# Odd projection of a hybrid decoder step: outputs stored in two runs a group, and a lighter hand-over to the next stage

## The chip, the cores and the metric

The program runs on one core of one Trainium2 chip. The metric is device time in microseconds (us) of one execution, lower is better; the kernel before takes 3164.81 us, the median of three runs.

## The reference, cut to what matters

One step of a two-layer decoder for 2048 prompt rows and 8 sample rows (2056 columns), D = 1024. The change lies in layer 1, at its input projection and the samples' stick-breaking attention:

```python
proj = x @ w_in                                  # x: 2056 rows of 1024
k_all = concat([cache_k[pages], k_new])          # 4096 past rows for each of 8 samples
z = q @ k_all.T / sqrt(64) + bias                # 8 heads
excl = exclusive_suffix_sum(log_sigmoid(-z))
att = exp(log_sigmoid(z) + excl)
o_c = att @ v_all
out = concat([o_c * silu(g_c), ...]) @ w_out
```

All is float32. The projection is computed as three float32r products of high and low parts.

## The kernel before, in words

`program` runs stages one after the other; each `Stage` ends with all engines at a barrier. Three classes of names matter: `po_` is the odd projection with the samples' attention (`project_odd`, L2448), `pv_` the next stage (`project_values`, L3049), `scratch_` and `out_` lie in device memory.

**The projection.** `Channels` (L1243) computes the transposed product in slots. A slot is one group of 128 output channels (`n`) times one block of 412 columns (`b`, five to a group; the last has 408). `ODD_GROUPS` (L2441) gives the order: slots 0 to 19 are broken up so that queries come early, and from slot 20 on each group's blocks 0 to 4 follow each other, so the block is the slot modulo 5. PE makes 24 matmuls a slot into one of five banks `acc`. ACT copies the bank to `ot` (`evict`, L1362), a buffer of four pieces of 412 columns that slots use in turn, and stores the piece (`store`, L1307). Before it overwrites a piece it waits until the store of four slots ago has landed (`stored`, L1313). There are 105 slots and 105 stores.

**The samples' attention** is spread over the same slots by a table written by hand (L2480 to L2490). Sample b (0 to 7) has its chain at slot c = 22 + 10b. DVE multiplies key pages with the query and reduces them, 16 pairs of pages a sample (`scores`). Then, in the order of the table: ACT takes `po_e` = exp (after its copy of slot c), DVE clamps, ACT takes the logarithm `po_softplus` (after slot c+1), DVE finishes `po_softplus`, PE makes the sums `po_stat` with a triangle and with ones (after slot c+2), DVE makes the argument, ACT takes `po_att` = exp (after slot c+3), and PE multiplies `po_att` with value pages into `po_sums`, from slot c+4 on, eight groups of four pages a sample.

**Queues.** SP issues the key pages. ACT issues the value pages (`load_pages`, L2493: for each page a register load from the page table, register arithmetic and one DMA), the output stores, and the weights of the projection. All this stands in ACT's one instruction stream, between its copies and exponentials. In the loop at L2596 a slot of ACT is: copy, store, weights at the first slot of a group, value pages, exponential or logarithm. POOL splits the weights of later groups into high and low parts.

**The hand-over.** After the last slot SP issues `ValuesAhead.load` (L2741): tile 0 of `pv_x`, four (`FRONT`) of the eight 512 KB parts of `pv_w`, and tile 1 of `pv_x`. Then it stores the samples' output `po_oc` to `scratch_cat` and waits until that has landed. In the next stage SP issues the other four parts, ACT makes `pv_w_high`, DVE first splits `pv_x` tile 0 (`split_x`, L2751) and then makes the eight `pv_w_low`; PE starts with part 0 and needs one part after the other. POOL makes the low half of tile 1, and PE goes on with it.

Of the kernel before, what the change touches and what calls it, by code (L numbers as in the profile page):

```python
# [22 lines left out]
P = 128  # L23
# [1219 lines left out]
class Channels:  # L1243
# [7 lines left out]
    def __init__(self, s, xT, w, out, groups, banks, pinned=False):  # L1251
# [14 lines left out]
        self.kept = [s.sem(f"kept{n}") for n in range(self.PIECES)]  # L1266
# [3 lines left out]
        for t, (i, n, b) in enumerate(self.slot):  # L1270
            self.begin.setdefault(i, t)
        self.opens = {t: i for i, t in self.begin.items()}
        self.at = {(n, b): t for t, (i, n, b) in enumerate(self.slot)}

    def place(self, stage=None):
        s = self.s
        if self.pinned:
            s.sb("fence", [P, 2 * KT * COLS])
        else:
            self.stage = stage  # L1280
            self.xh, self.xl = s.sb("x_high", [P, KT, COLS]), s.sb("x_low", [P, KT, COLS])
            self.wr = s.sb("w", [P, KT * P])
            self.wh, self.wl = s.sb("w_high", [P, 2, KT * P]), s.sb("w_low", [P, 2, KT * P])
        self.ot = s.sb("o", [P, self.PIECES, BLK])
        self.acc = [s.ps(f"acc{n}", [P, 512]) for n in range(self.banks)]

# [1161 lines left out]
def project_odd(nc, xT, w, z, cache_k, cache_v, table, bias, const, q_rows, cat, values_ahead):  # L2448
# [7 lines left out]
    with Stage(nc, "po") as s:  # L2456
# [16 lines left out]
         o_ev, o_pe, gate, out, stored) = (s.sem(n) for n in (  # L2473
             "cst", "tab", "q_tr", "q_ev", "q_st", "set", "prod", "k_used", "v_used", "biased", "exp", "cl", "ln",
             "sp", "tri_pe", "own", "arg", "att", "o_ev", "o_pe", "gate", "out", "stored"))
# [24 lines left out]
        def _(sp):  # L2500
# [33 lines left out]
            sp.dma_start(cat[0:4, :, SEQ:COLS].rearrange("n p c -> p n c"), oc[:, :, :]).then_inc(stored, 16)  # L2534
            sp.wait_ge(stored, 16)
# [51 lines left out]
        def _(act):  # L2587
# [8 lines left out]
            for t in range(TAIL):  # L2596
                if t < pj.slots:
# [6 lines left out]
                    pj.evict(act.copy, act, t, more)  # L2604
                    pj.store(act, t)
# [21 lines left out]
            for t in range(pj.slots - pj.PIECES, pj.slots):  # L2627
                pj.stored(act, t)

        @block.vector  # L2630
        def _(dve):
# [62 lines left out]
            for t in range(START, TAIL):  # L2694
# [10 lines left out]
                if t - PER - 3 in chain:  # L2705
# [4 lines left out]
                              gc[:, :, :].rearrange("p n b -> p (n b)"), ALU.mult).then_inc(out, 1)  # L2710

# [6 lines left out]
class ValuesAhead:  # L2718

    FRONT = 4  # L2720

    def __init__(self, nc, x, w):
# [9 lines left out]
        self.x_high, self.x_low = s.sem("x_high"), s.sem("x_low")  # L2732
# [8 lines left out]
    def load(self, sp):  # L2741
        self.tile(sp, 0)
        for k in range(self.FRONT):
            self.weights(sp, k)
        self.tile(sp, 1)
# [303 lines left out]
def project_values(nc, ahead, out, z, alpha_w, alpha_b, const, ops, wc, sample_vecs, scores):  # L3049
# [6 lines left out]
    with ahead.s as s:  # L3056
# [29 lines left out]
        def _(sp):  # L3086
# [13 lines left out]
            for k in range(ahead.FRONT, KT):  # L3100
                ahead.weights(sp, k)
            for dst, src in ((wt[:, :], alpha_w), (bt[:, :], alpha_b), (mask[:, :], const["reset"][:, 0:GW]),
# [27 lines left out]
            sp.wait_ge(late, 48)  # L3130
            for q in (0, 1):
# [104 lines left out]
        def _(dve):  # L3236
# [53 lines left out]
            ahead.split_x(dve)  # L3290
# [451 lines left out]
```

## Time and profile before

| | |
|---|---|
| median of three runs | 3164.81 us (3162.14 to 3166.29) |
| the profiled execution: its own time | 3165.45 us |
| its span in the profile | 3163.7 us |
| PE busy | 2913.2 us, 92% |
| DVE, ACT, POOL busy | 66%, 41%, 23% |
| stage `po`: first and last matmul of a slot | 1509.0 and 2124.2 us |
| first matmul of stage `pv` | 2141.12 us |

Times in the profile count from the span's start. "Idle" is time of an engine before an instruction, with what ended it. "issue" as a releaser means that the engine waited for nothing that the profile shows: its own instruction stream had other things ahead, here the issuing of DMAs. A granted clock (PEclk) of 1.00 is 2.4 GHz of TensorE, 0.50 is 1.2 GHz.

### The profile page before, as it was taken

Reading aid. Unit: us, or ns where it says so; the run is one execution under the profiler, and the core shown is the slowest. Engines: PE = TensorE matmul, PEld = TensorE weight load, DVE = VectorE, ACT = ScalarE, POOL = GpSimd, SP = SyncE. Lnnn points to the kernel's source line nnn. Section 1 sums busy time; section 2 is a strip of 40 time slices with the busy share of each in tenths; the row PEclk is TensorE's granted clock in tenths of the full one; section 3 lists DMA queues with packets and bytes.
Section 4 is the critical chain, followed back from the end, with each engine's and each line's share of the span. In section 5 each row is a group of like instructions: output and inputs, shape, how many; then the busy total and the mean of one; then the engine's idle time right before and its main releaser. Section 6 shows DMA issues by size and latency. Waiting matters only on the chain. (4 is left out here: it accounts for less than half of the span.)

```text
span 3163.7 us, 70060 instructions
## 1 busy us (share of the span) xinstructions
PE 2913.2 (92%) x27683; PEld 2367.9 (75%) x27683; DVE 2101.6 (66%) x3283; ACT 1291.1 (41%) x2293; POOL 724.9 (23%) x697
## 2 busy tenths in 40 slices
PE   8999999978898988998899999989989999998898
PEld 7899999967776766776887777877756666667676
DVE  9526666647666647885487677604639888887576
ACT  2225555434444435342310100012228888875332
POOL 5000000012232211110011111101227666664111
PEclk9999999989999989999999999999989999999999
DMA  6624545454443556552789999865450101008342
GB/s 214 204 95 151 154 151 153 140 162 117 105 116 87 130 150 195 158 174 84 260 253 342 319 330 322 294 192 170 149 193 6 68 14 55 15 20 257 124 158 77
DMA packets 470335, 502.83 MB, mean 159 GB/s; under 512 B 200065, under 2 KB 362866, under 8 KB 464986
## 3 DMA queue, kind: packets, MB, share of 16 engines
q1 hardware_dynamic: 373466, 339.83, 35.8%
q10 hardware_dynamic: 88032, 142.51, 13.0%
q0 software_dynamic: 8512, 16.02, 1.7%
q8 instruction: 221, 3.62, 0.5%
q14 instruction: 104, 0.85, 0.1%
HBM read 357.13 MB, written 141.31 MB: 158 GB/s over the span
## 5 line engine op out<-in xcount | busy, mean ns | idle before, releaser
L3029 POOL TENSOR_TENSOR sp_att<-sp_beta,sp_left 128x512 f32<-128x512 f32 (+3 forms) x320 | 302.3, 955 | 187.0 <-DVE sp_left L2990 172.6
L120 PE MATMUL po_acc<-po_x_high,po_w_low 128*128 128x412 f32 (+1 forms) x840 | 306.6, 365 | 15.1 <-DVE po_x_low L113 13.7
L120 PE MATMUL pe_acc<-pe_x_high,pe_w_low 128*128 128x412 f32 (+1 forms) x840 | 302.6, 360 | 5.4 <-PEq L86 5.4
L121 PE MATMUL po_acc<-po_x_low,po_w_high 128*128 128x412 f32 (+1 forms) x840 | 299.5, 357 | 0.0
L122 PE MATMUL po_acc<-po_x_high,po_w_high 128*128 128x412 f32 (+1 forms) x840 | 298.7, 356 | 0.0
L121 PE MATMUL pe_acc<-pe_x_low,pe_w_high 128*128 128x412 f32 (+1 forms) x840 | 293.7, 350 | 0.0
L122 PE MATMUL pe_acc<-pe_x_high,pe_w_high 128*128 128x412 f32 (+1 forms) x840 | 293.3, 349 | 0.0
L2990 DVE TENSOR_TENSOR_SCAN sp_left<-sp_z,sp_left,sp_zero 128x512 f32<-128x512 f32 x192 | 235.7, 1269 | 18.3 <-ACT sp_z L2951 14.0
L2654 DVE TENSOR_TENSOR po_work<-po_work,po_q 128x1024 f32<-128x1024 f32 x128 | 177.6, 1388 | 83.3 <-DMA po_work<-in_cache_k 74.4
L2943 ACT ACTIVATE sp_beta<-sp_z,sp_bias 128x512 f32<-128x512 f32 (+3 forms) x320 | 183.1, 628 | 94.1 <-PE sp_z L2881 47.7
L1371 ACT COPY po_o<-po_acc 128x412 f32<-128x412 f32 (+1 forms) x105 | 52.5, 500 | 392.2 <-PE po_acc L122 337.2
L120 PEld LDWEIGHTS po_acc<-po_x_high,po_w_low 128*128 128x128 f32 x840 | 162.4, 193 | 65.2 <-issue 33.1
L2430 POOL TENSOR_TENSOR rc_kt<-rc_kt,rc_mask 128x512 f32<-128x512 f32 x32 | 41.4, 1294 | 716.5 <-ACT rc_kt L2320 716.4
L2316 ACT COPY rc_lv<-rc_bk 128x1024 f32<-128x1024 f32 (+1 forms) x192 | 129.9, 693 | 181.1 <-DVE rc_f L2406 54.6
L2892 PEld LDWEIGHTS sp_t<-sp_id,sp_att 128*128 128x128 f32 x1088 | 117.4, 141 | 96.8 <-issue 89.8
L2951 ACT ACTIVATE sp_z<-sp_z,sp_bias_neg 128x512 f32<-128x512 f32 (+3 forms) x320 | 179.2, 610 | 0.0
L120 PEld LDWEIGHTS pe_acc<-pe_x_high,pe_w_low 128*128 128x128 f32 x840 | 158.4, 189 | 17.7 <-issue 16.5
L2878 PE MATMUL sp_z<-sp_k,sp_q 64*128 64x512 f32 (+3 forms) x640 | 164.0, 589 | 6.5 <-PEq L86 3.3
L2892 PE MATMUL sp_t<-sp_id,sp_att 128*128 128x128 f32 x1088 | 152.2, 279 | 17.5 <-ACT sp_aT L2957 16.6
L121 PEld LDWEIGHTS po_acc<-po_x_low,po_w_high 128*128 128x128 f32 x840 | 162.6, 194 | 0.9
L122 PEld LDWEIGHTS po_acc<-po_x_high,po_w_high 128*128 128x128 f32 x840 | 162.4, 193 | 0.7
L2909 PE MATMUL sp_ob<-sp_aT,sp_v 128*64 128x128 f32 x2176 | 154.7, 281 | 5.4 <-DVE sp_g L3004 5.4
(492 smaller groups left out, 6979.8 us busy)
## 6 DMA issues: line engine op xcount, KB each, us to landing
po_work<-in_cache_k SPq DMA_DIRECT2D x256, 256.0 KB, 4.8
po_work<-in_cache_v ACTq DMA_DIRECT2D x256, 256.0 KB, 4.6
scratch_ops<-pe_work SPq DMA_DIRECT2D x160, 128.0 KB, 2.0
out_z<-pe_o SPq DMA_DIRECT2D x84, 206.0 KB, 2.8
out_z<-po_o ACTq DMA_DIRECT2D x84, 206.0 KB, 4.2
pe_w<-in_w_e SPq DMA_DIRECT2D x21, 512.0 KB, 6.0
rc_opx<-scratch_ops SPq DMA_DIRECT2D x64, 160.0 KB, 3.7
po_w<-in_w_o ACTq DMA_DIRECT2D x20, 512.0 KB
```

Of the source, the lines that this page charges most:

```text
L120: pe.matmul(out, ll, rh, start=start, stop=False)
L121: pe.matmul(out, lh, rl, start=False, stop=False)
L122: return pe.matmul(out, lh, rh, start=False, stop=stop)
L2316: evict = lambda to, k, n: act.copy(lv[q][:, to:to + n].rearrange("p k x y c -> p x k (y c)"), b[:, :, 2 * k * CH:2 * (k + n) * CH].rearra ...
L2654: dve.tensor_tensor(kp[:, p % KR], kp[:, p % KR], qb[:, b % 2:b % 2 + 1, :].broadcast_to([P, 2, CW]), ALU.mult).then_inc(prod, 1)
L2878: mm[h] = pe.matmul(zb[h][b][:, 0:w], qt[q][r, cq], kt[q][r, ck], start=True, stop=not diagonal(n))
L2892: mm = pe.transpose(tb[h][:, b * P:(b + 1) * P], att[h][:, n % 3, b * P:(b + 1) * P], idt[:, :])
L2909: mm = pe.matmul(ob[tile(n) % 2][c, 0:P], vt[m % 2][:, 4 * g + b, c], aT[h][:, n % 2, b * P:(b + 1) * P], start=(diagonal(n) and b == 0), ...
L2943: act.activation(be[h][:, n % 4, 0:w], zb[h][n % 2][:, 0:w], ACT.Sigmoid, scale=DC ** -0.5, bias=bt[:, head:head + 1]).then_inc(sig[h], 1)
L2951: act.activation(zb[h][n % 2][:, 0:w], zb[h][n % 2][:, 0:w], ACT.Sigmoid, scale=-DC ** -0.5, bias=nbt[:, head:head + 1]).then_inc(kept[h], 1)
L2990: dve.tensor_tensor_scan(row[:, at:at + w][:, ::-1], zb[h][n % 2][:, 0:w][:, ::-1], zero.broadcast_to([P, w]), start, ALU.mult, ALU.add).t ...
L3029: pool.tensor_tensor(att[h][:, n % 3, 0:w], be[h][:, n % 4, 0:w], left[h][tile(n) % 2][:, at + 1:at + 1 + w], ALU.mult).then_inc(at_ok[h], 1)
```

## The change

- `ot` holds a whole row of 2056 columns in place of four pieces. A group is stored in two runs: blocks 0 and 1, and blocks 2 to 4. `store_run` stores a run after the copy of its last block; the copy of a block waits (`evict_run`) until the latest store that held the same block has landed. The broken-up groups give shorter runs. 45 stores take the place of 105, with the same bytes. The even projection, which shares the class, keeps its pieces.
- `FRONT` is 2, and tile 1 of `pv_x` is loaded behind the weights: six parts of `pv_w` and tile 1 are issued after the barrier, two parts and tile 0 before it.
- The landing of the samples' output is awaited at the end of the next stage (`cat_put`).
- DVE splits tile 0 of `pv_x` at the end of `po`.

```diff
-        self.ot = s.sb("o", [P, self.PIECES, BLK])
+        self.ot = s.sb("o", [P, self.PIECES, BLK] if self.pinned else [P, COLS])
...
+    def runs(self):
+        row, latest = [], {}
+        for t, (i, n, b) in enumerate(self.slot):
+            self.run_past[t] = latest.get(b)
+            row.append(b)
+            after = self.slot[t + 1] if t + 1 < self.slots else None
+            if after == (i, n, b + 1) and row != [0, 1]:
+                continue
+            count = self.run_count[row[0]] = self.run_count.get(row[0], 0) + 1
+            for x in row:
+                latest[x] = row[0], count
+            self.run_end[t] = row[0], b
+            row = []
+
+    def store_run(self, eng, t):
+        if t in self.run_end:
+            first, last = self.run_end[t]
+            lo, hi = first * BLK, min(COLS, (last + 1) * BLK)
+            eng.wait_ge(self.evicted, t + 1)
+            eng.dma_start(self.out[self.slot[t][1], :, lo:hi], self.ot[:, lo:hi]).then_inc(self.kept[first], 16)
...
+    def evict_run(self, copy, eng, t, more=()):
+        lo, hi = self.columns(t)
+        bank = self.acc[t % self.banks]
+        if self.run_past[t]:
+            first, count = self.run_past[t]
+            eng.wait_ge(self.kept[first], 16 * count)
+        eng.wait_ge(self.done, t + 1)
+        for dst in more:
+            copy(dst, bank[:, hi - lo - NS:hi - lo])
+        copy(self.ot[:, lo:hi], bank[:, 0:hi - lo]).then_inc(self.evicted, 1)
...
             sp.wait_ge(out, 1)
-            sp.dma_start(cat[0:4, :, SEQ:COLS].rearrange("n p c -> p n c"), oc[:, :, :]).then_inc(stored, 16)
-            sp.wait_ge(stored, 16)
+            sp.dma_start(cat[0:4, :, SEQ:COLS].rearrange("n p c -> p n c"), oc[:, :, :]).then_inc(values_ahead.cat_put, 16)
...
-                    pj.evict(act.copy, act, t, more)
-                    pj.store(act, t)
+                    pj.evict_run(act.copy, act, t, more)
+                    pj.store_run(act, t)
...
-            for t in range(pj.slots - pj.PIECES, pj.slots):
-                pj.stored(act, t)
+            pj.runs_stored(act)
...
                               gc[:, :, :].rearrange("p n b -> p (n b)"), ALU.mult).then_inc(out, 1)
+            values_ahead.split_x(dve)
...
-    FRONT = 4
+    FRONT = 2
...
             self.weights(sp, k)
-        self.tile(sp, 1)
...
             for k in range(ahead.FRONT, KT):
                 ahead.weights(sp, k)
+            ahead.tile(sp, 1)
...
             sp.wait_ge(late, 48)
+            sp.wait_ge(ahead.cat_put, 16)
...
-            ahead.split_x(dve)
             for k in range(KT):
                 ahead.low_w(dve, k)
```

ACT, from the exponential `po_e` of a sample (slot c) into slot c+1, whose block is 3: its copy, and the first of its four page loads. Before:

```order
L2616 ACTIVATE po_e<-po_scores 128x256
L1371 COPY po_o<-po_acc 128x412
L1310 DMA out_z<-po_o 128x412
L2495 TENSOR_LOAD po_pt
L2495 ISA x2
L2497 ISA
L2497 DMA po_work<-in_cache_v 128x512
```

The same place with the change:

```order
L2654 ACTIVATE po_e<-po_scores 128x256
L1324 COPY po_o<-po_acc 128x412
L2534 TENSOR_LOAD po_pt
L2534 ISA x2
L2536 ISA
L2536 DMA po_work<-in_cache_v 128x512
```

The store between the copy and the page loads is gone; in slot c (block 2) it is gone in the same way.

ACT, the last page load of slot c+2, then slot c+3, which opens a group (block 0) and ends with `po_att`. Before:

```order
L2497 DMA po_work<-in_cache_v 128x512
L1371 COPY po_o<-po_acc 128x412
L1310 DMA out_z<-po_o 128x412
L1294 DMA po_w<-in_w_o 128x1024
L2495 TENSOR_LOAD po_pt
```

And with the change:

```order
L2536 DMA po_work<-in_cache_v 128x512
L1324 COPY po_o<-po_acc 128x412
L1333 DMA po_w<-in_w_o 128x1024
L2534 TENSOR_LOAD po_pt
L2534 ISA x2
```

Here too the store between copy and loads is gone; it stands in slots c+2 (blocks 2 to 4, 1232 columns) and c+4 (blocks 0 and 1, 824 columns).

SP at the end of `po` and the start of `pv`; the branch is where the barrier stands. Before:

```order
L2736 DMA pv_x<-scratch_x1T 128x8x128
L2739 DMA pv_w<-in_w_v 128x1024 x4
L2736 DMA pv_x<-scratch_x1T 128x8x128
L2534 DMA scratch_cat<-po_oc 128x4x8
L84 UNCONDITIONAL_BRANCH
L3085 UNCONDITIONAL_BRANCH
L2739 DMA pv_w<-in_w_v 128x1024 x4
L3105 DMA pv_aw<-in_alpha_w 128x256
```

And with the change:

```order
L2774 DMA pv_x<-scratch_x1T 128x8x128
L2777 DMA pv_w<-in_w_v 128x1024 x2
L2573 DMA scratch_cat<-po_oc 128x4x8
L84 UNCONDITIONAL_BRANCH
L3122 UNCONDITIONAL_BRANCH
L2777 DMA pv_w<-in_w_v 128x1024 x6
L2774 DMA pv_x<-scratch_x1T 128x8x128
L3143 DMA pv_aw<-in_alpha_w 128x256
```

Two weight parts and tile 1 moved from before the barrier to behind it, and six parts now stand ahead of tile 1.

## Rows read from the trace of the kernel before

**Rows 1.** Windows view, sample attention: width, busy times, PEclk, DMA share, GB/s.

```profile
1640.00:2040.00 400.00, 377.23 (x2045) 313.96 (x2044) 294.94 (x256) 39.44 (x88) 47.97 (x25) 0.97 0.94 322
```

**Rows 2.** Waits view, 1600 to 2126 us: total us, times, longest.

```profile
DVE po_work L2654 <- DMA po_work<-in_cache_k: 70.1, 54, 3.4
DVE po_e L2668 <- ACT po_e L2616: 34.1, 6, 17.1
DVE po_softplus L2673 <- ACT po_softplus L2620: 22.8, 7, 5.3
PE po_stat L2559 <- DVE po_softplus L2673: 15.5, 8, 6.5
PE po_sums L2552 <- ACT po_att L2625: 14.7, 7, 2.9
PE po_sums L2552 <- DMA po_work<-in_cache_v: 1.9, 2, 1.1
```

**Rows 3.** Timeline, ACT, sample 4: start us, us, instruction, idle before it.

```profile
1873.07 0.48 ACT L1371 COPY po_o<-po_acc 128x412 f32<-128x412 f32 x1
1873.58 0.36 ACTq L1310 DMA_DIRECT2D out_z<-po_o  x1
1874.65 3.61 ACTq L2497 DMA_DIRECT2D po_work<-in_cache_v  x4
1878.36 0.42 ACT L2620 ACTIVATE po_softplus<-po_e 128x256 f32<-128x256 f32 x1 [4.81 <-issue]
...
1892.68 0.42 ACT L2625 ACTIVATE po_att<-po_scores 128x256 f32<-128x256 f32 x1 [5.43 <-issue]
```

**Rows 4.** Timeline, DVE and PE, the same sample.

```profile
1878.81 0.99 DVE L2673 TENSOR_TENSOR po_softplus<-po_softplus,po_scores 128x256 f32<-128x256 f32 x1 [2.93 <-ACT po_softplus L2620]
...
1879.86 0.70 PE L2559 MATMUL po_stat<-po_softplus,po_tri 128*128 128x256 f32 x2 [1.51 <-DVE po_softplus L2673]
...
1893.15 1.05 PE L2552 MATMUL po_sums<-po_work,po_att 128*8 128x512 f32 x8 [2.02 <-ACT po_att L2625]
```

**Rows 5.** Windows view, `po_sums` start to end of next slot; samples 1, 4, 7.

```profile
1706.20:1715.98 9.78, 9.78 (x44) 8.48 (x48) 7.20 (x7) 0.34 (x1) 0.00 (x0) 0.65 0.73 257
1893.15:1901.33 8.18, 8.18 (x44) 6.92 (x48) 5.47 (x6) 0.33 (x1) 0.00 (x0) 0.79 0.95 342
2079.44:2086.06 6.62, 6.62 (x44) 5.49 (x48) 0.00 (x0) 0.34 (x1) 0.00 (x0) 1.00 0.24 81
```

**Rows 6.** Timeline, ACT, near the end of the kernel.

```profile
2924.13 0.51 ACT L3500 COPY gc_opx<-gc_raw 64x384 f32<-64x384 f32 x1
2924.14 0.37 ACTq L3517 DMA_DIRECT2D scratch_o_d<-gc_ot  x1
```

**Rows 7.** Tile view of `po_o`, us from issue to landing of its stores.

```profile
DMA to landing us min/median/max: 2.7/4.3/8.2
```

**Rows 8.** Windows view around the barrier (columns as in rows 1).

```profile
2126.00:2136.00 10.00, 1.05 (x8) 0.97 (x8) 0.49 (x2) 1.10 (x2) 0.00 (x0) 0.74 1.00 337
```

**Rows 9.** Timeline, SP, the samples' output store.

```profile
2128.35 2.85 SPq L2534 DMA_DIRECT2D scratch_cat<-po_oc  x1
```

**Rows 10.** Waits view, SP, at the barrier: total us, times, longest.

```profile
SPq L84 <- DMA scratch_cat<-po_oc: 5.4, 1, 5.4
```

**Rows 11.** Timelines of DVE, PE and POOL after the barrier.

```profile
2137.89 0.69 DVE L108 CAST pv_x_high<-pv_x 128x1024 fp32r<-128x1024 f32 x1 [10.26 <-PEq L86]
2138.62 1.23 DVE L113 TENSOR_TENSOR pv_x_low<-pv_x,pv_x_high 128x1024 fp32r<-128x1024 f32 x1
2139.76 9.17 DVE L113 TENSOR_TENSOR pv_w_low<-pv_w,pv_w_high 128x1024 fp32r<-128x1024 f32 x8
...
2141.12 0.77 PE L120 MATMUL pv_acc<-pv_w_high,pv_x_low 128*128 128x512 f32 x1 [13.72 <-DVE pv_w_low L113]
...
2150.01 2.39 POOL L113 TENSOR_TENSOR pv_x_low<-pv_x,pv_x_high 128x1024 fp32r<-128x1024 f32 x1 [80.96 <-DVE pv_x_high L108]
```

**Rows 12.** Tile view of `pv_w`, us from issue to landing.

```profile
DMA to landing us min/median/max: 3.6/5.8/7.3
```

More of the change, by code:

```diff
@@ L1265, in __init__ @@
         self.done, self.evicted = s.sem("done"), s.sem("evicted")
-        self.kept = [s.sem(f"kept{n}") for n in range(self.PIECES)]
+        self.kept = [s.sem(f"kept{n}") for n in range(self.PIECES if pinned else NBLK)]
         self.slot = [(i, n, b) for i, (n, blocks) in enumerate(groups) for b in blocks]
@@ L1271, in __init__ @@
             self.begin.setdefault(i, t)
+        self.run_end, self.run_past, self.run_count = {}, {}, {}
+        if not pinned:
+            self.runs()
         self.opens = {t: i for i, t in self.begin.items()}
@@ L1283, in place, with runs_stored @@
             self.wh, self.wl = s.sb("w_high", [P, 2, KT * P]), s.sb("w_low", [P, 2, KT * P])
-        self.ot = s.sb("o", [P, self.PIECES, BLK])
+        self.ot = s.sb("o", [P, self.PIECES, BLK] if self.pinned else [P, COLS])
         self.acc = [s.ps(f"acc{n}", [P, 512]) for n in range(self.banks)]
+    def runs(self):
[17 more added lines that the diff above has]
+            eng.dma_start(self.out[self.slot[t][1], :, lo:hi], self.ot[:, lo:hi]).then_inc(self.kept[first], 16)
+    def runs_stored(self, eng):
+        for first, count in self.run_count.items():
+            eng.wait_ge(self.kept[first], 16 * count)
[4 more added lines that the diff above has]
+            first, count = self.run_past[t]
+            eng.wait_ge(self.kept[first], 16 * count)
+        eng.wait_ge(self.done, t + 1)
+        for dst in more:
+            copy(dst, bank[:, hi - lo - NS:hi - lo])
+        copy(self.ot[:, lo:hi], bank[:, 0:hi - lo]).then_inc(self.evicted, 1)
     def columns(self, t):
@@ L2472, in project_odd @@
         (cst, tab, q_tr, q_ev, q_st, set_, prod, k_used, v_used, biased, exp_, cl, ln, spl, tri_pe, own_, arg, att_ok,
-         o_ev, o_pe, gate, out, stored) = (s.sem(n) for n in (
+         o_ev, o_pe, gate, out) = (s.sem(n) for n in (
              "cst", "tab", "q_tr", "q_ev", "q_st", "set", "prod", "k_used", "v_used", "biased", "exp", "cl", "ln",
-             "sp", "tri_pe", "own", "arg", "att", "o_ev", "o_pe", "gate", "out", "stored"))
+             "sp", "tri_pe", "own", "arg", "att", "o_ev", "o_pe", "gate", "out"))
         k_in, v_in = [s.sem(f"k_in{n}") for n in range(KR)], [s.sem(f"v_in{n}") for n in range(VR)]
@@ L2731, in __init__ @@
         self.w_low, self.x_in = [s.sem("w_low_even"), s.sem("w_low_odd")], [s.sem("x_in0"), s.sem("x_in1")]
-        self.x_high, self.x_low = s.sem("x_high"), s.sem("x_low")
+        self.x_high, self.x_low, self.cat_put = s.sem("x_high"), s.sem("x_low"), s.sem("cat_put")
     def tile(self, sp, t):
```

## Prediction

> **What bounds the kernel now.** I read the windows view first. While the samples' attention runs, PE is busy 377 of 400 us at a granted clock of 0.97 [rows 1]; it is the bound, and what can be gained in this stage is PE's idle time and the time at the lower clock. The waits view says who ends PE's waits [rows 2]: the sums `po_stat` wait 15.5 us in all for DVE's `po_softplus` (8 times, the longest 6.5), the first product of each sample waits 14.7 us in all for ACT's `po_att` (7 times), and 1.9 us go to value pages. DVE in turn waits 22.8 us for ACT's logarithm. So both chains lead to ACT.
>
> ACT computes little. Its timeline [rows 3] shows what it does: copy at 1873.07, the store issued at 1873.58, the first page load only at 1874.65, four loads until 1878.26, and right behind them the logarithm at 1878.36, idle before it "<-issue". DVE had waited 2.93 us for it, and PE 1.51 us for DVE [rows 4]. The same holds for `po_att`: it stands right behind four page loads, and PE waited 2.02 us for it [rows 3, 4]. In seven of the eight samples an instruction that PE needs stands behind issues on ACT. In the first sample DVE itself is late (the wait of 6.5 us), and nothing here touches that.
>
> The second place is the barrier to the next stage. The DMA engines are full from 2126 to 2136 [rows 8], SP waits 5.4 us for the samples' output to land [rows 10], and PE stands still for 13.7 us [rows 11].
>
> **The change part by part.**
>
> *ACT's stores.* 60 of 105 go. From slot 20 on they go in blocks 0, 2 and 3, and the samples' chains start at block 2. So there is no store ahead of the exponential, none ahead of the logarithm, and none ahead of `po_att`. What is a missing store worth on ACT? The issue is 0.36 us. But the store also waited for the copy to end (0.48 us), since it reads what the copy writes; page loads need not wait for the copy. Near the end of the kernel a DMA is issued 0.01 us after a copy has started, with the copy still running [rows 6], so ACT's instruction stream goes on while its datapath works. Page loads begin with a load of a register, which no row shows beside a running copy. So one store is worth between 0.4 us (issue alone) and 0.9 us (1873.07 to 1873.94). I take 0.9, because the row nearest to it shows the overlap.
>
> The Trainium skill (Perfetto Trace Analysis, on the lifecycle of a DVE / Act engine instruction) has the sequencer ready for the next instruction once one is in the wait queue; by that it is 0.9. If a register load waited for an empty datapath it would be 0.4, and the sum below would be some 11 us smaller.
>
> *The logarithm.* It gains 0.9 in its own slot, and up to 0.4 more where the exponential made the copy of slot c+1 late. `po_softplus` then comes 0.9 to 1.3 us earlier, and it also gets ahead of POOL's weight split, beside which it took 0.99 us. The waits other than the first are 15.5 - 6.5 = 9.0 us; seven waits of about 1.3 us are covered by that shift. I take 8.7. At 0.4 a store it is about 4.
>
> *`po_att`.* Seven waits, each shorter by 0.9: 6.3 us (2.8 at 0.4). 8.4 us of them stay, since the four page loads still stand ahead.
>
> *Value pages.* They are issued 0.9 us earlier at block 2, where the two late groups start: of 1.9 us I take 1.3. A run of 616 KB goes ahead of other groups' pages in the same queue; those groups start behind a block 4.
>
> *The clock.* From the start of `po_sums` to the end of the next slot PE takes 8.18 us at a mean clock of 0.79 in sample 4, and 6.62 at 1.00 in sample 7, for the same 44 matmuls; sample 1 takes 9.78 [rows 5]. Samples 2, 3 and 5 are as 4, and 6 is as 1. So the fall costs 4 x 1.56 + 2 x 3.16 = 12.6 us. Sample 7's wait was 1.28 us, the others' 1.8 to 2.9, with the fall right behind them. Shorter by 0.9, four of the six come under 1.28. Whether that keeps the clock up is uncertain: bounds 0 and 12.6, and I take half, 6.3.
>
> *The wait for a store's landing.* Block 2 may be copied when the run of blocks 2 to 4 of the group before has landed, three slots after its issue, at least 3 x 4.5 = 13.4 us. Stores of 206 KB landed after 4.3 us, at most 8.2 [rows 7]. 410 KB more, at half of the 322 GB/s of rows 1, are 2.5 us, so 10.7 at most: no wait. In the broken-up slots 5, 6 and 7 the same columns are stored three times running, and ACT waits for each landing, some 4 us; PE has five banks and does not come to wait. Cost 0, hidden by those banks.
>
> *The barrier.* Before, 3.37 MB pass from 2126 to 2136 [rows 8] and then the barrier opens. Moved behind it are 1.5 MB (two parts, tile 1); 0.4 MB come ahead of it with the last run. The new last comers are DVE's split (tile 0 and the last run, 1.1 MB from 2126 on at the 337 GB/s of rows 8, are through at 2129.4, with 1 us to land 2130.5; then 0.69 + 1.23 us [rows 11]) and the last run. Both give about 2132.5, against 2136.6 when the 5.4 us wait of rows 10 ended: 4.1 us earlier. SP no longer issues tile 1 there; the store's issue of 2.85 us [rows 9] stays and ends by 2130.6.
>
> Behind it, with B as the start of `pv`: before, the last `pv_w_low` ended at B + 11.1 and POOL's low half of tile 1 at B + 14.5 (2152.40), ahead of PE, which reached tile 1 at about B + 15.7. Now DVE starts without the split, PE starts at B + 2.3 in place of 3.3, and would reach tile 1 at B + 14.7. The first of six parts lands 3.6 us after its issue [rows 12], the others 1.3 us apart, the last at B + 9.9; cast and split put it at B + 12.2, in time. Tile 1 lands near B + 12.5, DVE 0.7 and POOL 2.4 us later it is ready at B + 16.0. So PE waits 1.3 us there, and of 4.1 us 3.8 stay. Bounds 1.5 and 5.5.
>
> The Trainium skill (DMA: Bandwidth & Descriptors, Queues, rings and completion order) lets an engine drain a whole packet of 9 to 17 descriptors of one queue before it turns to the other. By that the last run's rows would all pass ahead of tile 0 wherever they meet, and tile 0 and DVE's split would come late by as much; the barrier's gain would still be within the bounds above, as both are counted as through together.
>
> **Sum.** 8.7 + 6.3 + 1.3 + 6.3 + 3.8 = 26.4 us, from the profiled execution's own 3165.45: 3139.0. That execution lies 0.6 us above the median, which I leave.
>
> **Rivals.**
>
> *Half a saving* (the change does not do on ACT what I say: page loads start only when the copy has ended). 4 + 2.8 + 0.5 + 3 + 3.8 = 14 us: 3151. For it: no row shows a register load beside a copy.
>
> *Key pages become the bound.* The DMA share is 0.94, and DVE waits 70.1 us for key pages. If PE runs faster, DVE must deliver faster, and PE's waits come back as waits for DVE. Against: DVE has 34.1 + 22.8 us of waiting for ACT [rows 2] to give up first, more than the 15 us wanted. Then the barrier and little else stay: 3160.
>
> *Landings hold ACT up: slower.* Place: the copy of block 2, slot c. Point: a landing of 13.4 us. If thrice the bytes take 16.4 us behind page loads, ACT is 3 us late at every sample's exponential and logarithm, 8 x 3 = 24 us, against some 10 of `po_att` and barrier: 3179. For it: in that queue a run lies behind up to eight page loads, and rows 7 show 8.2 at worst. Against: 10.7 as worked out.
>
> **Chances.** Forecast 0.60, half a saving 0.17, key pages 0.12, landings 0.06, no change at all for reasons not seen 0.05. 0.2% is 6.3 us, about what a measurement of this kernel can tell from no change. Faster: 0.60 + 0.17 + about half of 0.12 = 0.83; within: 0.11; slower 0.06. Low end: 9.0 + 6.3 + 1.9 + 12.6 + 5.5 = 35.3, so 3130. High end: half a saving without the clock, with the barrier at 1.5, is 4 + 2.8 + 1.5 = 8.3, so 3157, stretched to 3159 toward the key-page case.
>
> **What the profile should show.** 45 stores from ACT; the first page load about 0.7 us after the copy's start in blocks 2 and 3, not 1.6; `po_stat` waiting only in the first sample; `po_att` waits near 1.2 us each; fewer falls of PEclk between 1700 and 2030; the first matmul of `pv` some 5 us sooner after the last slot, and a short PE wait for POOL before tile 1. I am wrong if the first page load still comes over 1 us after the copy's start, if ACT waits "<-DMA out_z<-po_o" from slot 20 on, or if DVE's waits for key pages grow by what its waits for ACT shrink and more.

## The result, and the profile after

| | before | changed |
|---|---|---|
| median of four runs each | 3163.47 us (3162.11 to 3166.29) | 3129.36 us (3125.2 to 3135.5) |
| span of the profiled execution | 3163.7 us | 3130.5 us |

The ratio of the times is 0.9893, with a 95% interval of 0.9872 to 0.9913. The forecast was 3139.0 in a range of 3130 to 3159, so the direction held, the gain was 34 us in place of 26, and the time lies 0.6 us below the range. The forecast was reckoned from the profiled execution's own 3165.45 us, which lies 2.0 us above the median of the table; 2.0 of the 9.6 us between forecast and time are that.

Three numbers split the spans. The samples' stage, from its first matmul to the start of the last of the eight `po_outp` matmuls, took 618.1 us (1509.04 to 2127.15) and now takes 584.6 (1509.04 to 2093.60). From there to PE's first matmul on tile 1 of `pv_x` it was 26.5 us and is 23.0. All that follows takes 3.8 us more. The stage is thus where the gain is: 33.5 us, where the prediction has 22.6. PE's last output matmuls and its first on tile 1, before and then changed; the last of the eight starts at 2127.15 and 2093.60:

```profile
2126.35 1.05 PE L2565 MATMUL po_outp<-po_ones,po_om 128*128 128x1 f32 x8 [0.81 <-DVE po_om L2690]
2153.62 0.39 PE L120 MATMUL pv_acc<-pv_w_high,pv_x_low 128*128 128x512 f32 x1
...
2092.80 1.05 PE L2603 MATMUL po_outp<-po_ones,po_om 128*128 128x1 f32 x8 [0.81 <-DVE po_om L2727]
2116.59 0.50 PE L120 MATMUL pv_acc<-pv_w_high,pv_x_low 128*128 128x512 f32 x1
```

Waits view of the changed kernel, 1600 to 2095 us, as [rows 2]:

```profile
DVE po_work L2691 <- DMA po_work<-in_cache_k: 71.1, 56, 3.7
...
DVE po_e L2705 <- ACT po_e L2654: 14.2, 2, 13.3
DVE po_softplus L2710 <- ACT po_softplus L2658: 12.1, 5, 5.4
...
PE po_sums L2590 <- ACT po_att L2663: 5.4, 7, 1.1
PE po_stat L2597 <- DVE po_softplus L2710: 4.9, 1, 4.9
```

PE's waits for `po_stat` fell from 15.5 to 4.9 us, and the one that is left is the first sample's. Those for `po_att` fell from 14.7 to 5.4, that is by 1.3 us a sample in the mean of seven (0.9 to 2.1). The two waits for value pages are gone. DVE waits for key pages as long as before (71.1 against 70.1 us); what it gave up are its waits for ACT, 56.9 to 26.3 us.

Windows view of the changed kernel: the attention of the samples, then three stretches from the start of `po_sums` to the end of the next slot (samples 1, 4 and 7), as [rows 1, 5]:

```profile
1640.00:2009.00 369.00, 363.94 (x2046) 303.12 (x2046) 287.69 (x253) 40.14 (x88) 48.84 (x26) 1.00 0.98 347
1704.16:1710.80 6.64, 6.64 (x44) 5.50 (x48) 4.00 (x5) 0.34 (x1) 0.00 (x0) 1.00 1.02 384
1875.46:1882.10 6.64, 6.64 (x44) 5.51 (x48) 3.84 (x4) 0.34 (x1) 0.00 (x0) 1.00 1.05 401
2045.93:2052.60 6.67, 6.67 (x44) 5.53 (x48) 0.00 (x0) 0.34 (x1) 0.00 (x0) 1.00 0.30 110
```

Sample 1 took 9.78 us for the same 44 matmuls at a granted clock of 0.65, and sample 4 took 8.18 at 0.79. Both now take 6.64 at 1.00. None of the six falls behind `po_att` is left, which is the whole 12.6 us.

Timeline of ACT in sample 4 of the changed kernel, as [rows 3]:

```profile
1857.81 0.51 ACT L1324 COPY po_o<-po_acc 128x412 f32<-128x412 f32 x1 [0.93 <-PE po_acc L122]
1858.51 3.55 ACTq L2536 DMA_DIRECT2D po_work<-in_cache_v  x4
1862.15 0.42 ACT L2658 ACTIVATE po_softplus<-po_e 128x256 f32<-128x256 f32 x1 [3.84 <-issue]
...
1870.01 0.50 ACT L1324 COPY po_o<-po_acc 128x412 f32<-128x412 f32 x1 [6.04 <-PE po_acc L122]
1870.03 0.35 ACTq L1333 DMA_DIRECT2D po_w<-in_w_o  x1
1871.09 3.79 ACTq L2536 DMA_DIRECT2D po_work<-in_cache_v  x4
1874.99 0.42 ACT L2663 ACTIVATE po_att<-po_scores 128x256 f32<-128x256 f32 x1 [4.48 <-issue]
```

The first page load starts 0.70 us after the copy's start, where it was 1.58. That is the step on which the value of a store hung, and it is 0.9 us as taken. The Trainium skill (Perfetto Trace Analysis, in the lifecycle of a DVE / Act engine instruction) has the sequencer ready for the next instruction as soon as one is in the wait queue, and the trace agrees: 0.70 us is less than the copy's 0.51 and a register load's 0.29 together.

`po_att` gains more. The timeline of ACT before, at the same place of sample 4, and then the first register load of sample 1 there, before and changed (views of L2495 and L2534):

```profile
1886.75 0.50 ACT L1371 COPY po_o<-po_acc 128x412 f32<-128x412 f32 x1 [7.58 <-PE po_acc L122]
1887.28 0.35 ACTq L1310 DMA_DIRECT2D out_z<-po_o  x1
1887.67 0.44 ACTq L1294 DMA_DIRECT2D po_w<-in_w_o  x1
1889.08 3.50 ACTq L2497 DMA_DIRECT2D po_work<-in_cache_v  x4
...
L2495 ACTq TENSOR_LOAD <-po_pt x1: 1070/1070/1070, 1700.6 to 1700.6; - x1
L2534 ACTq TENSOR_LOAD <-po_pt x1: 286/286/286, 1699.4 to 1699.4; - x1
```

The weights' DMA started 0.93 us after the copy's start and now starts at 0.02: that is the same 0.9. But its issue took 0.44 us and takes 0.35, and the first register load behind it, which took 0.5 to 1.1 us in five of the seven samples, takes 0.3 in all seven.

Tile view of `po_o`:

```profile
DMA to landing us min/median/max: 2.6/6.4/10.6
```

The longest landing is 10.6 us, against 8.2 before [rows 7] and a deadline of 13.4.

Timelines of SP, DVE and PE at the barrier of the changed kernel, as [rows 9, 11]. SP's six weight parts are the first thing behind it:

```profile
2094.11 0.39 SPq L2573 DMA_DIRECT2D scratch_cat<-po_oc  x1
...
2097.47 0.69 DVE L108 CAST pv_x_high<-pv_x 128x1024 fp32r<-128x1024 f32 x1 [3.39 <-DMA pv_x<-scratch_x1T]
2098.20 1.23 DVE L113 TENSOR_TENSOR pv_x_low<-pv_x,pv_x_high 128x1024 fp32r<-128x1024 f32 x1
...
2100.55 2.79 SPq L2777 DMA_DIRECT2D pv_w<-in_w_v  x6
...
2103.01 0.77 PE L120 MATMUL pv_acc<-pv_w_high,pv_x_low 128*128 128x512 f32 x1 [9.16 <-DVE pv_w_low L113]
...
2114.14 2.39 POOL L113 TENSOR_TENSOR pv_x_low<-pv_x,pv_x_high 128x1024 fp32r<-128x1024 f32 x1 [75.94 <-DVE pv_x_high L108]
```

DVE's split ends at 2099.43 and the barrier opens (read here and below as SP's first DMA behind it) 1.1 us later, 6.95 us behind the last `po_outp` (2093.60; it was 10.7). PE reaches tile 1 at 2116.59, 0.06 us after POOL had it ready.

### The profile page after: what moved, and what is told of

It reads as the page before. It is cut to its first block and busy times, and to the rows that moved or that the text cites. A ratio compares the mean times of both kernels' runs of the same rounds, so it can differ in the third digit from the quotient of the medians.

```text
span 3130.5 us, 69998 instructions
## 1 busy us (share of the span) xinstructions
PE 2912.7 (93%) x27683; PEld 2369.4 (76%) x27683; DVE 2100.5 (67%) x3283; ACT 1292.1 (41%) x2293; POOL 725.7 (23%) x697
## 5 line engine op out<-in xcount | busy, mean ns | idle before, releaser
L121 PEld LDWEIGHTS pe_acc<-pe_x_low,pe_w_high 128*128 128x128 f32 x840 | 158.8, 189 | 1.3
```

Of the source, the lines that this page charges most:

```text
L121: pe.matmul(out, lh, rl, start=False, stop=False)
```

## The experiments

Each kernel is the changed one with the edit shown, where nothing else is said. "Stage" is the samples' stage and "hand-over" the stretch from the last `po_outp` to tile 1, as above: 618.1 and 26.5 us before, 584.6 and 23.0 changed. Ratios are to the kernel before on the same chip, with their intervals.

### The two parts by themselves

Runs alone: the projection's stores are as changed, the hand-over as before.

```diff
-    FRONT = 2
+    FRONT = 4
...
+        self.tile(sp, 1)
...
+            sp.wait_ge(values_ahead.cat_put, 16)
...
-            values_ahead.split_x(dve)
...
-            ahead.tile(sp, 1)
...
+            ahead.split_x(dve)
```

> Stores in two runs a group, hand-over as before (four weight parts and tile 1 ahead of the barrier, the samples' output awaited there, split in the next stage). Theory A (the store's place in ACT's stream, and with it the clock): stage po from 1509.0 to its last po_outp matmul takes 585 us as with the whole change (before 618), from there to tile 1 of pv 26.5 us as before; total near 3133. Rival B (most of the stage's gain comes with the hand-over, or is chance): po near 600 or more, total over 3145.

3131.96 us, ratio 0.9885 (0.9866 to 0.9903). Stage 575.8, hand-over 29.6, where the theory had 26.5. The `po_att` waits are those of the whole change, 5.3 us in all, and one clock fall begins between 1510 and 2080:

```profile
PE po_sums L2591 <- ACT po_att L2664: 5.3, 7, 1.1
PE po_stat L2598 <- DVE po_softplus L2711: 0.9, 2, 0.5
```

The first sample's wait is nearly gone too (0.4 us). That wait differs from one kernel's profile to the next, for a reason that was not found (below), and with the clock fall beside it, it is most of the 9 us by which this stage is shorter than the changed kernel's. The profiled execution was also the fastest of this kernel's four, and that of the changed kernel the second slowest. So stages of single profiles are compared here by their waits and falls, and a few us between their totals show nothing.

Hand-over alone: the stores are as before.

```diff
-                    pj.evict_run(act.copy, act, t, more)
-                    pj.store_run(act, t)
+                    pj.evict(act.copy, act, t, more)
+                    pj.store(act, t)
```

> Stores as before (105 pieces), hand-over as in the change. Theory A: po takes 618 us as before, last po_outp to tile 1 of pv 23.0 us in place of 26.5; total near 3160. Rival B (the hand-over and the runs need each other, since the last run's landing ends the stage): the hand-over alone gives 4.5 us or more, as its last store is 204 KB in place of 616 KB; total near 3158.

3159.46 us, ratio 0.9973 (0.9963 to 0.9984). Stage 621.5, hand-over 21.4. Its waits in the stage are those of before. There is a fall behind each of the seven `po_att`, and one more behind a wait of 2.1 us for value pages:

```profile
PE po_stat L2595 <- DVE po_softplus L2709: 15.3, 8, 7.4
PE po_sums L2588 <- ACT po_att L2661: 14.6, 7, 2.8
```

So the stores carry nearly all of the gain. The hand-over alone is worth 0.3% by the ratio, some 8.5 us, and 5.1 us in its own stretch of the profile. That is the rival's 4.5 or more. DVE's split ends 4.4 us behind the last `po_outp` there and 5.8 in the changed kernel; tile 0 of `pv_x` lands at 2.5 there (2.3 before) and at 3.6 to 4.0 in the kernels with runs. The rival puts this to the size of the last store, which was not tried by itself. The merged stores thus cost the hand-over something: 1.6 us with its changes (23.0 against 21.4) and 3.1 without (29.6 against 26.5).

### Is it the place of the store, or its size?

The kernel before, with all 105 small stores, each issued at the end of its slot on ACT, behind page loads and activations:

```diff
                     pj.evict(act.copy, act, t, more)
-                    pj.store(act, t)
...
+                if t < pj.slots:
+                    pj.store(act, t)
```

> The kernel before, with all its 105 stores and their size, but ACT issues a slot's store behind its page loads and its exponential or logarithm instead of right behind the copy. Theory A (what counts is what stands between the copy and the exponential on ACT, 0.9 us with the wait for the copy): PE's waits for po_softplus other than the first go, those for po_att fall from 14.7 to about 6 us, PEclk does not fall between 1700 and 2050; po takes 586 us, total near 3134. Rival C (fewer and larger packets relieve the DMA engines, and pages come sooner): po stays at 618, total near 3163.

3138.13 us, ratio 0.9899 (0.9882 to 0.9917). Stage 587.0, and the `po_att` waits are 5.4 us, as in the changed kernel:

```profile
PE po_stat L2559 <- DVE po_softplus L2674: 8.2, 5, 6.7
PE po_sums L2552 <- ACT po_att L2624: 5.4, 7, 1.1
```

There is no fall between 1640 and 2097. The size of the stores is not what matters, nor their number as such: it is what stands on ACT between a copy and what PE waits for.

### One store a group

```diff
-            if after == (i, n, b + 1) and row != [0, 1]:
+            if after == (i, n, b + 1):
```

> The changed kernel with one store a group (the row of blocks 0 to 4, 1 MB) in place of two. 40 stores in place of 45 and more. Theory (landings are short against three slots, but not against one): block 0 of the next group is copied one slot (some 6.7 us) after the store's issue, and 1 MB lands after 10 us or more, so ACT waits 4 to 8 us for the landing at each block 0; PE has five banks and may not come to wait at once, but ACT's logarithm or po_att two or three slots later comes late: slower than the changed kernel by 5 to 40 us. Rival (landings don't matter here, since only the number of ACT's instructions does): as the changed kernel or faster by 1 to 3 us.

3136.08 us, where the changed kernel, run again on the same chip, took 3125.14. Stage 590.1. Waits view, 1600 to 2095, ACT and PE:

```profile
ACT po_o L1324 <- DMA out_z<-po_o: 79.3, 12, 8.1
...
PE po_sums L2590 <- ACT po_att L2663: 9.4, 7, 2.8
```

ACT waits for a landing twelve times, up to 8.1 us. This is the prediction's slow rival, and its mechanism exists: with a deadline of one slot it costs 11 us. With three slots, as in the change, it costs nothing: the changed kernel has no such wait from 1600 us on.

### po_att between the page loads

In slot c+3 ACT issues two of the four page loads, then `po_att`, then the other two.

```diff
+                halves = slice(0, 4) if t - 3 not in chain else slice(0, 2)
...
-                        values(g + VR)
+                        values(g + VR, halves)
...
                     act.activation(flat(att), flat(zs[b % 2]), ACT.Exp).then_inc(att_ok, 1)
+                    for g in at(groups, t - 1):
+                        if g + VR < NS * GROUPS:
+                            values(g + VR, slice(2, 4))
```

> The whole change, and po_att issued after two of the four page loads of its slot instead of behind all four. Theory A (ACT's issues still hold po_att up by 5.4 us in all): those waits go, po takes 579 us, total 5 us under the change. Rival D (the stage is now bound by data: the DMA share is 0.98, and the two later page loads, 0.4 us later, or DVE's argument come late): PE waits for value pages or for po_att take their place, total as with the change within 2 us.

3117.16 us, ratio 0.9837 (0.9808 to 0.9866), on the chip where runs alone took 3131.96. Stage 573.9. No wait for `po_att` is left in the waits view, nor a fall between 1520 and 2082:

```profile
PE po_stat L2597 <- DVE po_softplus L2714: 3.4, 3, 1.5
```

So the `po_att` waits that the change left, 5.4 us (the prediction left 8.4 standing), were to be had by the same means. They are all that this profile shows for the edit: of the stage's 10.6 us under the changed kernel, 3.4 are the first sample's wait, and some 4 are two clock falls, at 1548 and 1634 us, that are not there; both lie ahead of sample 1. The ratio is the lowest of all, though its interval just overlaps that of the changed kernel run again (below). With the split behind the barrier as well, `po_att` in the middle and `po_att` behind its loads gave 0.9866 and 0.9867, so what the edit is worth in the whole kernel stays open.

### How long may PE wait before the clock falls?

The changed kernel once more, and with register loads that do nothing (about 0.5 us each, and no other work) on ACT ahead of `po_att`, ahead of the logarithm, or both:

```diff
+                    for _ in range(2):
+                        act.value_load(pt[0:1, 0:1], min_val=0, max_val=cache_v.shape[0] - 1)
                     act.activation(flat(att), flat(zs[b % 2]), ACT.Exp).then_inc(att_ok, 1)
```

> The changed kernel once more, as the partner of this batch. Profiled before: 3130.5 us span, the samples' stage 584.6 us from its first matmul to the start of the last po_outp, then 23.0 us to tile 1 of pv, seven po_att waits of 5.4 us in all, and no fall of the granted clock between 1700 and 2030. In the kernel with runs alone the first sample's po_stat wait was 0.5 us and the stage 575.8 us. If that was chance of the execution, this one shows either of the two again; if the hand-over's change costs the first sample its cover, the wait of 4.9 us is here again.

> The changed kernel with one register load more (about 0.7 us) on ACT ahead of po_att in every sample. po_att's seven waits (0.5 to 1.1 us in the changed kernel) become 1.2 to 1.8 us each, 5 us in all more. Theory (a PE wait of 1.8 us or more brings the clock fall, one up to 1.28 us does not): the waits lie between the two bounds, so that some falls may come: the stage 590 to 600 us. Rival (the falls have nothing to do with this wait): 5 us more and no fall, 590 us.

> As att_late1, with two register loads more (about 1.4 us). Theory: po_att's waits become 1.9 to 2.5 us, as in the kernel before, and with them the falls of the granted clock behind them come back: about 10 us of waits and 9 to 12.6 us of clock, the stage 604 to 608 us, the kernel near 3152. Rival (the clock has nothing to do with these waits): 10 us of waits alone, the stage 595 us, the kernel near 3141, and the granted clock 1.00 behind po_att.

> The changed kernel with three register loads more on ACT ahead of the logarithm and two ahead of po_att (each about 0.5 us, by the two kernels with loads ahead of po_att). With two ahead of po_att alone PE waited 1.4 to 2.1 us at each po_att, and the granted clock fell behind the waits of 2.00 and 2.12 us and behind none of the five of 1.42 to 1.83, while in the kernel before it fell behind one of 1.82 that had a po_stat wait of 1.8 us some 13 us ahead of it. Theory (a fall needs both waits of a sample): po_stat waits near 1.5 us come back in most samples, and with them falls behind five to seven of the seven po_att waits; 10 us of clock more than with po_att late alone, and 8 us of waits: the kernel near 3158. Rival (po_att's wait alone decides, from 2.0 us on): the po_stat waits come back and at most three falls; near 3149.

> The changed kernel with three register loads more on ACT ahead of the logarithm alone. With these and two ahead of po_att the po_stat waits of 1.5 us came back, and the granted clock fell behind four of the seven po_att waits of 1.7 to 2.1 us, without them behind two of seven. Theory (PE's idle time of a sample as a whole decides: 1.5 and 0.8 us here, about as much as 1.8 us of po_att alone, which was followed by a fall only in two of seven): zero to two falls, 5 to 8 us of waits, the kernel 5 to 10 us above the changed one. Rival (the po_stat wait is what brings the fall, wherever po_att stands): four falls or more, 12 us of clock and the waits, some 20 us above.

The changed kernel again: 3125.14 us, ratio 0.9867 (0.985 to 0.9883), stage 582.6, hand-over 22.7. The first sample's wait of 5.0 us was there again, with one fall behind a `po_att`. The four others, with each sample's waits from PE's timeline and falls that begin within 2.5 us of the start of `po_sums`:

| | time, ratio | stage | po_stat waits, samples 1 to 7 | po_att waits | falls |
|---|---|---|---|---|---|
| one load ahead of po_att | 3132.63, 0.9893 | 587.0 | none to 0.4 | 0.9 to 1.6 | 2 of 7 |
| two ahead of po_att | 3141.29, 0.9919 | 594.4 | none | 1.4 to 2.1 | 2 of 7 |
| three ahead of the logarithm | 3137.93, 0.991 | 594.6 | 1.5 to 1.8 | 0.3 to 1.0 | 0 of 7 |
| both | 3154.81, 0.9957 | 611.1 | 1.5 to 1.8 | 1.7 to 2.1 | 4 of 7 |
| kernel before | 3163.47 | 618.1 | 0.6 to 1.8 | 1.3 to 2.9 | 6 of 7 |

Waits view, 1600 to 2095: two ahead of `po_att`, then three ahead of the logarithm, then both.

```profile
PE po_sums L2590 <- ACT po_att L2665: 12.8, 7, 2.1
PE po_stat L2597 <- DVE po_softplus L2712: 4.8, 1, 4.8
```

```profile
PE po_stat L2597 <- DVE po_softplus L2712: 15.5, 8, 4.6
PE po_sums L2590 <- ACT po_att L2665: 5.3, 7, 1.0
```

```profile
PE po_stat L2597 <- DVE po_softplus L2714: 15.7, 8, 4.8
PE po_sums L2590 <- ACT po_att L2667: 12.9, 7, 2.1
```

Against the changed kernel run again, two loads ahead of `po_att` cost 11.8 us of stage: 7.3 of waits (12.8 against 5.5), and two falls where the other has a shorter one. With both waits late it is 28.5: 7.4 and 10.7 of waits, and for most of the rest the clock, three falls of 3.2 us and one of 1.6.

With two loads the theory had falls as before and 3152 us, the rival no fall and 3141; the time is the rival's (3141.29), but there are two falls. With both late, the theory had five to seven falls and 3158 us, the rival at most three and 3149; four falls and 3154.8 lie between them. The kernel with the late logarithm cost 12.8 us in place of 5 to 10, since each of its seven `po_stat` waits came to 1.5 or more.

No single profile settles what brings a fall, but all of them together say more. These are the 98 `po_att` waits of the 14 profiles that have them (all but the three with `po_att` in the middle), and how many were followed by a fall:

| wait for `po_att`, us | `po_stat` wait of the sample 1.5 or more | shorter or none |
|---|---|---|
| 0.34 to 1.17 | 1 of 10 | 5 of 51 |
| 1.26 to 1.85 | 6 of 10 | 1 of 12 |
| 1.99 to 2.91 | 6 of 6 | 9 of 9 |

Two of the nine are of the kernel with one store a group, where the first sample alone had a `po_stat` wait:

```profile
1816.18 1.08 PE L2590 MATMUL po_sums<-po_work,po_att 128*8 128x512 f32 x8 [2.36 <-ACT po_att L2663]
1934.96 0.63 PE L2590 MATMUL po_sums<-po_work,po_att 128*8 128x512 f32 x4 [2.80 <-ACT po_att L2663]
```

So a `po_att` wait of 2.0 us or more was followed by a fall every time, whether the sample had a `po_stat` wait or not. Waits of 1.80 to 1.83 us alone were not (none of four), which refutes the theory's 1.8. Between 1.26 and 1.85 the `po_stat` wait beside it makes the difference, 6 of 10 against 1 of 12, and a `po_stat` wait of 1.5 to 1.8 with a short `po_att` wait brings hardly any (1 of 10). Both rivals on record fail in part: the falls have to do with these waits, and waits under 2.0 us can bring them too. What decides within a group stays open. With both late the falls came behind samples 1, 3, 5 and 7, every second one, though the waits hardly differ; where in time a wait lies seems to matter, and no run tried it.

### The hand-over taken apart

The awaited store, the split, and the parts, each put back alone:

```diff
+            sp.wait_ge(values_ahead.cat_put, 16)
```

> The changed kernel with the samples' output store awaited ahead of the barrier again, and nothing else. From the start of the last po_outp to tile 1 of pv the changed kernel takes 23.0 and 22.7 us, the kernel before 26.5. Theory (DVE's split of tile 0, which ends 6 us behind the last po_outp, is the last comer at the barrier, and the store lands near it): 0.5 to 1.5 us more, 24 us. Rival (the wait was what held the barrier): 3 to 4 us more, 26.5 us.

```diff
-            values_ahead.split_x(dve)
...
+            ahead.split_x(dve)
```

> The changed kernel with DVE's split of tile 0 back behind the barrier. Theory (the split is the last comer at the barrier; behind it DVE does the same work at the same time, while SP's six weight parts can go out 1.9 us earlier): the first matmul of pv within 0.5 us of the changed kernel's 9.2 us behind the last slot, tile 1 at 21.5 to 23 us. Rival (the split ahead of the barrier is what the hand-over gains): the first matmul 1.9 us later, tile 1 at 25 us.

```diff
-    FRONT = 2
+    FRONT = 4
...
+        self.tile(sp, 1)
...
-            ahead.tile(sp, 1)
```

> The changed kernel with four weight parts and tile 1 ahead of the barrier, as before the change (1.5 MB more there). At the 337 GB/s of the stretch ahead of the barrier that is 4.5 us. Theory (the bytes ahead of the barrier set when it opens): the first matmul of pv 3.5 to 4.5 us later, tile 1 3 to 4 us later, 26.5 us in all, so that this part is all of the hand-over's gain. Rival (the parts behind the barrier make tile 1 late by as much): no difference at tile 1.

And two on top of `po_att` in the middle: with the split behind the barrier, and with that and the parts as before.

> The changed kernel with po_att between the page loads (the kernel that gave 0.9837) and DVE's split of tile 0 behind the barrier. Theory (the two gains lie in different places and add): 2.3 us less from the last po_outp to tile 1 than the 22.7 us of po_att in the middle alone, 20.4 us; the samples' stage 574 us; the kernel near 3112 to 3115. Rival (the split's place gained only by chance of that execution): 22 to 23 us to tile 1.

> As mid_split, with four weight parts and tile 1 ahead of the barrier again; of the hand-over's changes only the store that isn't awaited is left. With the split ahead of the barrier, four parts there cost nothing at tile 1 (22.1 us against 22.7 and 23.0), since the split ended last. Theory (with the split gone the bytes ahead of the barrier are what ends last): the barrier opens 2 to 4 us later than in mid_split, tile 1 at 22 to 24 us. Rival (the bytes never decide, only the awaited store behind them did): tile 1 at 20 us, as in mid_split, so that the parts' place gave nothing.

All times in us from the last `po_outp`; where the split ends later than the barrier opens, it stands behind it:

| | DVE's split ends | store lands | barrier opens | tile 1 | time, ratio |
|---|---|---|---|---|---|
| before | 12.7 | 9.4 | 10.7 | 26.5 | |
| changed | 5.8 | 6.7 | 6.95 | 23.0 | 3129.36, 0.9893 |
| hand-over alone | 4.4 | 5.4 | 5.6 | 21.4 | 3159.46, 0.9973 |
| store awaited | 5.8 | 6.5 | 7.8 | 23.7 | 3130.44, 0.9875 |
| split behind | 6.5 | 6.5 | 4.55 | 20.4 | 3122.77, 0.9867 |
| four parts, tile 1 ahead | 5.6 | 10.7 | 6.7 | 22.1 | 3130.86, 0.9888 |
| runs alone (all three) | 15.0 | 11.8 | 13.0 | 29.6 | 3131.96, 0.9885 |
| po_att in the middle | 5.8 | 6.5 | 6.9 | 22.7 | 3117.16, 0.9837 |
| and split behind | 7.0 | 6.6 | 5.0 | 22.1 | 3120.14, 0.9866 |
| and four parts, tile 1 ahead | 9.5 | 11.5 | 7.5 | 23.75 | 3120.59, 0.9856 |

The times of whole kernels can hardly tell these apart (the intervals are 0.004 to 0.007 wide); the profiles, one of each, can as far as a difference is clear of the 0.3 us between the two of the changed kernel (23.0 and 22.7 to tile 1). Timeline of SP, four parts ahead; then of runs alone; then of the last line of the table:

```profile
2092.40 2.82 SPq L2777 DMA_DIRECT2D pv_w<-in_w_v  x4
...
2095.83 3.78 SPq L2573 DMA_DIRECT2D scratch_cat<-po_oc  x1
2101.03 1.80 SPq L2777 DMA_DIRECT2D pv_w<-in_w_v  x4
```

```profile
2081.76 5.03 SPq L2573 DMA_DIRECT2D scratch_cat<-po_oc  x1
2093.15 1.76 SPq L2777 DMA_DIRECT2D pv_w<-in_w_v  x4
```

```profile
2085.04 4.62 SPq L2573 DMA_DIRECT2D scratch_cat<-po_oc  x1
2090.91 1.78 SPq L2780 DMA_DIRECT2D pv_w<-in_w_v  x4
```

- With the split ahead of the barrier, four parts and tile 1 there cost nothing: it opens at 6.7, since the split ends last in both, and tile 1 comes 0.9 us sooner. The theory (3 to 4 us later) is refuted.
- The wait alone costs 0.7 to 1 us, as the theory had it. Behind four parts and tile 1 it costs far more: the store's issue takes 3.8 to 5.0 us in place of 0.4, it lands 9 to 10 us after the issue's start, and with the wait the barrier opens at 13.0, without it (last line, which also has `po_att` in the middle) at 7.5.
- The split ahead of the barrier holds it up: without it the barrier opens at 4.55 (no view tells what comes last then). The first matmul came 1.6 us sooner (7.8 against 9.4) and tile 1 2.6, more than either the theory (21.5 to 23 us to tile 1) or the rival (25) had. On top of `po_att` in the middle the first matmul still came 1.1 us sooner, but tile 1 only 0.6, so the gain there is between the theory's 2.3 and the rival's nothing. The whole kernel took 3120.1 us, not the theory's 3112 to 3115.
- With the split gone and four parts ahead, the barrier opens at 7.5, and 1.25 us before that SP ends the store's issue of 4.62 us. The last comer is most likely that issue: wherever the split or the awaited landing comes last, the barrier opens 1.1 to 1.3 us behind it. That is 2.5 us later than with two parts, and tile 1 comes 1.6 us later, as the theory had it. So the queue of parts does cost something once the split is out of the way.

Timeline of SP and DVE, split behind:

```profile
2082.50 0.39 SPq L2573 DMA_DIRECT2D scratch_cat<-po_oc  x1
...
2086.54 2.78 SPq L2776 DMA_DIRECT2D pv_w<-in_w_v  x6
...
2086.57 0.69 DVE L108 CAST pv_x_high<-pv_x 128x1024 fp32r<-128x1024 f32 x1 [4.10 <-PEq L86]
```

## Why the prediction was right in kind and too small

| term | predicted | measured in the profiles |
|---|---|---|
| logarithm, `po_stat` waits | 8.7 | 10.6 (15.5 to 4.9) |
| `po_att` waits | 6.3 | 9.3 (14.7 to 5.4) |
| value pages | 1.3 | 1.9 (none left) |
| clock | 6.3 | 12.6 |
| hand-over | 3.8 | 3.5 |
| sum | 26.4 | 37.9 |

From the 37.9 us come off 1.2 of a longer gap at 1548 us and 3.8 in the stages behind the hand-over, which the edit does not touch; that leaves 32.9 of the 33.2 between the spans.

- **The clock** is the step that failed. The text gave bounds of 0 and 12.6 and took the middle, 6.3, since "whether that keeps the clock up is uncertain"; all of it came. The rest of the prediction pointed there: it forecast `po_att` waits near 1.2 us, and the one wait of its rows without a fall was 1.28. They came to 0.4 to 1.1 us. Over all profiles 6 of 61 waits that short were followed by a fall, and all 15 of 2.0 us or more, the kind that five of the six falls before stood behind. The sixth had 1.8 us and a `po_stat` wait of 1.8 ahead of it. So the shorter `po_att` waits are enough to account for five of the falls; for the sixth both waits may count.
- **po_att** gained 9.3 us and not 6.3. What the store itself held up was 0.9 us, as taken. The other 3 us are the weights' issue and the first register load behind it, which took 0.5 to 1.1 us in five of seven samples before and 0.3 after. They are short with the stores last as well, and long again in four of seven samples of the hand-over alone. Why they are long behind a store and the weights was not tried.
- **The logarithm**: the waits other than the first went completely, 9.0 us where 8.7 were taken. The working was too generous: five of the seven waits were 1.5 to 1.8 us, and a shift of 1.3 covers 7.6 us of the seven. For the rest, DVE's finish of `po_softplus` took 0.43 us in the median where it had taken 0.71; the text named that gain without a price. The first wait, taken as untouched, shrank by 1.6. It is unlikely that the change moved it: in the 14 profiles of kernels with runs it is 4.6 to 5.0 us in nine, and 4.0, 1.5, 1.5, 0.4 and 0.2 in the others, one of which (1.5) differs from the changed kernel only in the split behind the barrier, 450 us later. What moves it was not tried.
- **The landings** (10.7 predicted, 10.6 measured), the **key pages** (71.1 us of waits against 70.1) and the overlap of page loads with a copy came as forecast, so the rivals "half a saving", "key pages" and "landings" fell.
- **The hand-over** came out at nearly the right size for partly the wrong reason. The place of the split's end was right (5.3 worked out, 5.8 measured), and so was that the store's wait goes. But the moved bytes, on which the working rested, decide nothing while the split ends last: the queue of parts made the awaited store late, and either fewer parts or no wait would have done. The store's issue, taken to stay at 2.85 us, fell to 0.39. The split ahead of the barrier was a loss, and the merged stores cost 1.6 us there. That the sum of these came out at 3.5 us is in part luck. PE's wait of 1.3 us before tile 1 was 0.06, and 0.98 in the second profile.
- **The range** was the last fault: its low end took every term at its upper bound except `po_att`, which had none above 6.3. With 9.3 there it would have been 3127; from the median of the result in place of the profiled execution, 3128, and the time would have lain within.

## What to carry to other kernels

On an engine that computes little and issues much, price a DMA by what it stands in front of, and not by its issue time: a store that reads what the copy before it writes also makes every later issue wait for the copy. Moving the same 105 stores to the end of their slots gave nearly the gain of merging them. When a wait of the matmul engine is brought down to a length that no fall of the clock follows in the rows, count the whole fall as won and not half of it. And before work is placed ahead of a barrier, ask which engine arrives last there.

## What the runs showed of the hardware

- Page loads run beside a copy: the first DMA of four, with its register load and arithmetic, starts 0.70 us after the start of a 0.5 us copy; a DMA without them starts 0.02 us after it.
- The samples' output store behind four 512 KB loads and the second 512 KB tile in one queue took 2.9 to 5.0 us to issue (five profiles) and 8.2 to 10.1 to land, against 0.4 and 4.9 to 7.0 behind two parts and one tile.
- A register load on ACT took 0.29 us in the median (288 ns over the 244 of 1600 to 2126 us before), but 0.5 to 1.1 in five of the six slots of `po_att` where it stood behind an output store and the weights' DMA.
- The granted clock fell from 2.4 to 1.2 GHz behind all 15 `po_att` waits of 1.99 to 2.91 us, behind 6 of 10 of 1.28 to 1.85 that had a `po_stat` wait of 1.5 or more some 13 us ahead, behind 1 of 12 as long without it, and behind 6 of 61 of 0.34 to 1.17. A fall cost 1.6 or 3.2 us in a stretch that takes 6.6 at full clock.
